# Attention of a fused two-layer mixer: the first query block in two visits of four heads per group, the second in four visits of two

## What is computed

```python
# 8 heads in 2 groups of 4, head width 64; one key and value head per group
q = rotary(zq) * Dh ** -0.5
p_c = masked_softmax(q @ k_c.T, mask_c) * mask_c          # 31 compressed keys
o_cmp = p_c @ v_c
# "selected" branch: 16 of 8 blocks, so all causal keys; "window" branch: window 512, so all causal keys
o_slc = softmax(q @ k_slc.T + causal) @ v_slc
o_win = softmax(q @ k_win.T + causal) @ v_win
g = sigmoid(zg)
o = g[..., 0:1] * o_cmp + g[..., 1:2] * o_slc + g[..., 2:3] * o_win
```

## Time and profile before

| | |
|---|---|
| median of three runs | 2074.64 us (2074.2 to 2075.43) |
| the profiled execution's own time | 2072.95 us |
| its span, first to last instruction | 2071.1 us |
| TensorE matmul busy | 2043.2 us, 99% of the span |
| VectorE busy | 1209.7 us, 58% |
| ScalarE busy | 685.6 us, 33% |
| GpSimd busy | 917.5 us, 44% |
| mean granted TensorE clock | 0.997 |

### The profile page before, as it was taken

One profiled execution on the slowest core, in us unless ns is written; L12 is line 12 of the kernel. 1 busy time (PEld: TensorE's weight loads), 2 busy tenths in 40 slices (PEclk: granted clock), 3 DMA queues, 4 the chain that ended last, 5 costly groups with the idle time before them and its releaser, 6 DMA issues.

```text
span 2071.1 us, 31913 instructions
## 1 busy us (share of the span) xinstructions
PE 2043.2 (99%) x9800; PEld 1637.2 (79%) x9800; DVE 1209.7 (58%) x1799; ACT 685.6 (33%) x1007; POOL 917.5 (44%) x672
## 2 busy tenths in 40 slices
PE   9999999999999999999999999999999999999997
PEld 7777677888888888888887777778888888888886
DVE  7766865422327888862267677572322378888522
ACT  4355533323232322222233554333323232222222
POOL 3422233444445555545544212335444455555552
PEclk9999999999999999999999999999999999999998
DMA  5311132222232223223233112322223223232233
GB/s 210 99 60 52 55 91 91 96 92 101 91 101 92 96 97 101 92 94 111 93 126 96 53 51 64 95 89 95 101 91 101 91 93 101 92 101 96 100 105 108
DMA packets 57432, 194.90 MB, mean 94 GB/s; under 512 B 7040, under 2 KB 7552, under 8 KB 57216
## 3 DMA queue, kind: packets, MB, share of 16 engines
q1 hardware_dynamic: 52576, 186.17, 26.8%
q10 hardware_dynamic: 4768, 7.61, 1.5%
HBM read 186.67 MB, written 2.10 MB: 91 GB/s over the span
## 4 chain that ended last, share of the span: by engine, by line
PE 93%; DVE 4%; issue 1%; ACT 1%; DMA 0%; ACTq 0%; SPq 0%; DVEq 0%
PE acc L1189 28%; PE acc L1191 28%; PE acc L1190 28%; PE o L1389 2%; PE s L1363 2%; PE t L1371 1%; PE o L1428 1%; PE s L1418 1%; PE t L1409 0%; DVE win_k L779 0%; DMA w_raw<-weights_dram 0%; PE s L1444 0%; PE s L1435 0%; DVE rstd L752 0%; DVE sc L721 0%
## 5 line engine op out<-in xcount | busy, mean ns | idle before, releaser
L434 POOL TENSOR_TENSOR w_lo<-w_raw,w_hi 128x512 fp32r<-128x512 f32 x668 | 917.3, 1394 | 1129.6 <-ACT w_hi L456 1114.0
L1189 PE MATMUL acc<-xg_hi,w_hi 128*128 128x512 f32 x1904 | 769.5, 404 | 6.5 <-DVE sc L721 3.6
L1191 PE MATMUL acc<-xg_hi,w_lo 128*128 128x512 f32 x1904 | 742.9, 390 | 0.0
L1190 PE MATMUL acc<-xg_lo,w_hi 128*128 128x512 f32 x1904 | 741.8, 390 | 0.0
L456 ACT ACTIVATE w_hi<-w_raw 128x1024 fp32r<-128x1024 f32 x336 | 355.1, 1057 | 777.5 <-PE acc L1191 740.3
L1189 PEld LDWEIGHTS acc<-xg_hi,w_hi 128*128 128x128 f32 x1904 | 357.4, 188 | 116.5 <-issue 33.4
L1190 PEld LDWEIGHTS acc<-xg_lo,w_hi 128*128 128x128 f32 x1904 | 357.8, 188 | 77.1 <-issue 6.7
L1191 PEld LDWEIGHTS acc<-xg_hi,w_lo 128*128 128x128 f32 x1904 | 357.3, 188 | 76.4
L1066 DVE TENSOR_TENSOR work<-acc,rstd 128x512 f32<-128x512 f32 x64 | 44.1, 690 | 256.1 <-PE acc L1191 256.1
L1189 PE MATMUL acc<-act_hi,w_hi 128*128 128x512 f32 x352 | 136.9, 389 | 0.0
L1190 PE MATMUL acc<-act_lo,w_hi 128*128 128x512 f32 x352 | 136.9, 389 | 0.0
(11 more groups left out here) (208 smaller groups left out, 2238.1 us busy)
## 6 DMA issues: line engine op xcount, KB each, us to landing
w_raw<-weights_dram SPq DMA_DIRECT2D x339, 512.0 KB, 3.3
x<-xT_dram SPq DMA_DIRECT2D x8, 256.0 KB, 5.9
rot<-rq ACTq DMA_DIRECT2D x16, 128.0 KB
rot<-rk ACTq DMA_DIRECT2D x16, 128.0 KB
dec<-decay_dram ACTq DMA_DIRECT2D x8, 256.0 KB, 3.3
out_dram<-x SPq DMA_DIRECT2D x8, 256.0 KB, 2.7
con<-consts_dram SPq DMA_DIRECT2D x1, 1406.0 KB, 10.5
w1k<-w_dram SPq DMA_DIRECT2D x2, 512.0 KB, 8.7
```

The costliest lines, as they stand in the source:

```text
L434: nc.gpsimd.tensor_tensor(w_lo[:, slot, part], w_raw[:, slot, part], w_hi[:, slot, part].bitcast(F32), ALU.subtract).then_inc(lo_ready, 1)
L1189: mm(tile, w_h, right_hi, start=first, stop=False)
L1190: mm(tile, w_h, right_lo, start=False, stop=False)
L1191: return mm(tile, w_l, right_hi, start=False, stop=last)
```

## The change

The pairs of one head give way to `VISITS`, each with a list of heads `js`. Block 0 has two visits of four heads per group, block 1 four visits of two, blocks 2 and 3 eight visits of one as before: 22 visits a layer, where there were 32. The steps of a visit are 4 slots apart in block 0, 3 in block 1, 2 in blocks 2 and 3. A group's heads lie side by side in one bank, so one `s` bank, one `t` bank and one copy to `pT` serve up to 512 columns. The count of products, transposes, exponentials and scalings stays, that of VectorE's copies and of its gate steps falls. `scores` on TensorE now waits for both banks before its first product. The last attention step moves from slot 73 to slot 62.

```diff
+VISITS = [(_qi, _br, tuple(range(_j, _j + _n))) for _qi, _n in ((0, 4), (1, 2), (2, 1), (3, 1))
+          for _j in range(0, 4, _n) for _br in range(2)]
+STEP = {0: 4, 1: 3, 2: 2, 3: 2}
...
-    if _n == 0:
-        _e += [("scores", 0), ("scores", 1)]
-    if _n % 2 and _n < UNITS:
-        _e.append(("scale", _n - 1))
-    if _n % 2 and 3 <= _n < UNITS + 2:
-        _e += [("turn", _n - 3), ("turn", _n - 2)]
-    if _n % 2 and _n >= 5:
-        _e.append(("values", _n - 5))
-    if _n % 2 and _n + 1 < UNITS:
-        _e += [("scores", _n + 1), ("scores", _n + 2)]
+STEP_SLOT = [4]
+for _qi, _, _ in VISITS:
+    STEP_SLOT.append(STEP_SLOT[-1] + STEP[_qi])
+STEP_SLOT += [STEP_SLOT[-1] + 2, STEP_SLOT[-1] + 4]
+for _i, _n in enumerate(STEP_SLOT):
+    if _i < len(VISITS) and (_i == 0 or VISITS[_i][0] != VISITS[_i - 1][0]):
+        _qi = VISITS[_i][0]
+        _at = _n + (0 if _qi else 1)
+        SIDE[_at].append(("cmp_scores", _qi))
+        SIDE[_at + 2].append(("cmp_scale", _qi))
+        SIDE[_at + 4].append(("cmp_turn", _qi))
+    if 1 <= _i <= len(VISITS):
+        SIDE[_n].append(("scale", _i - 1))
+    if 2 <= _i <= len(VISITS) + 1:
+        SIDE[_n].append(("turn", _i - 2))
+    if 3 <= _i:
+        SIDE[_n].append(("values", _i - 3))
+        if _i == len(STEP_SLOT) - 1 or VISITS[_i - 2][0] != VISITS[_i - 3][0]:
+            SIDE[_n].append(("attn_hi", VISITS[_i - 3][0]))
+            SIDE[_n + 2].append(("attn_lo", VISITS[_i - 3][0]))
+    if _i < len(VISITS):
+        SIDE[_n].append(("scores", _i))
...
-        def pr_of(u):
-            return (pr, pr_odd)[u // 2 % 2][:, u % 2, 0:(unit(u)[0] + 1) * P]
+        def pr_of(v, g):
+            return (pr, pr_odd)[v % 2][:, g, :]
...
-                                u = e[1]
-                                act.wait_ge(s_free, 1 + s_use(L, e) + 1)
-                                nc.scalar.activation(pr_of(u), pr_of(u), ACT.Exp, bias=nmax[:, u % 2:u % 2 + 1], scale=-1.0,
-                                                     accum_out=den[:, u % 4:u % 4 + 1]).then_inc(a_made, 1)
+                                qi, _, js = VISITS[e[1]]
+                                w = (qi + 1) * P
+                                for g in range(KV_GROUPS):
+                                    act.wait_ge(s_free, 1 + s_use(L, (*e, g)) + 1)
+                                    for i in range(len(js)):
+                                        part, c = pr_of(e[1], g)[:, i * w:(i + 1) * w], g * len(js) + i
+                                        ins = nc.scalar.activation(part, part, ACT.Exp, bias=nmax[:, c:c + 1], scale=-1.0,
+                                                                   accum_out=den[:, c:c + 1])
+                                    ins.then_inc(a_made, 1)
...
-                    u = e[1]
-                    w = (unit(u)[0] + 1) * P
-                    s_wait(e)
-                    alone(dve)
-                    s_end(ve.tensor_tensor_reduce(pr_of(u), s_of(e)[:, 0:w], C("causal", S)[:, S - w:S],
-                                                  -(DH ** -0.5), 3e38, ALU.add, ALU.min, nmax[:, u % 2:u % 2 + 1]), e)
+                    qi, _, js = VISITS[e[1]]
+                    w = (qi + 1) * P
+                    for g in range(KV_GROUPS):
+                        name = (*e, g)
+                        s_wait(name)
+                        alone(dve)
+                        for i in range(len(js)):
+                            c = g * len(js) + i
+                            ins = ve.tensor_tensor_reduce(pr_of(e[1], g)[:, i * w:(i + 1) * w], s_of(name)[:, i * w:(i + 1) * w],
+                                                          C("causal", S)[:, S - w:S], -(DH ** -0.5), 3e38, ALU.add, ALU.min, nmax[:, c:c + 1])
+                        s_end(ins, name)
 
                 def scale(e):
 
-                    u = e[1]
-                    qi, br, j = unit(u)
-                    sums, out_ = den[:, u % 4:u % 4 + 2], scl[:, u % 4:u % 4 + 2]
-                    dve.wait_ge(a_made, a_count(L, ("scores", u + 1)))
-                    then(ve.reciprocal(out_, sums))
-                    g2 = gates[:, qi, :].rearrange("p (g h b) -> p b h g", g=2, b=3)[:, 1 + br, j, :]
-                    v_end(ve.tensor_tensor(out_, out_, g2, ALU.mult), e)
+                    qi, br, js = VISITS[e[1]]
+                    n = KV_GROUPS * len(js)
+                    out_ = scl[e[1] % 2][:, 0:n]
+                    dve.wait_ge(a_made, a_count(L, ("scores", e[1], 1)))
+                    then(ve.reciprocal(out_, den[:, 0:n]))
+                    g2 = gates[:, qi, :].rearrange("p (g h b) -> p b g h", g=2, b=3)[:, 1 + br, :, js[0]:js[0] + len(js)]
+                    out3 = out_.rearrange("p (g h) -> p g h", g=2)
+                    v_end(ve.tensor_tensor(out3, out3, g2, ALU.mult), e)
 
                 def turn(e):
-                    u = e[1]
-                    w = (unit(u)[0] + 1) * P
-                    t_wait(e)
-                    if u >= 2:
-                        dve.wait_ge(pv_done, pv_count(L, ("values", u - 2)))
-                    t_end(ve.tensor_copy(pT[:, u % 2, 0:w], t_of(e)[:, 0:w]), e)
+                    qi, _, js = VISITS[e[1]]
+                    w = (qi + 1) * P * len(js)
+                    for g in range(KV_GROUPS):
+                        t_wait((*e, g))
+                        if e[1]:
+                            dve.wait_ge(pv_done, pv_count(L, ("values", e[1] - 1, g)))
+                        t_end(ve.tensor_copy(pT[:, g, 0:w], t_of((*e, g))[:, 0:w]), (*e, g))
...
-                    qi, br, h = unit(e[1])
+                    qi, br, js = VISITS[e[1]]
                     w = (qi + 1) * P
-                    r = slice(64 * (h // 4), 64 * (h // 4) + 64)
-                    b = s_begin(e)
+                    banks = [s_begin((*e, g)) for g in range(KV_GROUPS)]
                     last_wait()
-                    mm(b[:, 0:w], qT[r, h % 4, qi * P:(qi + 1) * P], kT[r, br, 0:w], start=True, stop=True).then_inc(s_done, 1)
+                    for i, j in enumerate(js):
+                        for g in range(KV_GROUPS):
+                            r = slice(64 * g, 64 * g + 64)
+                            ins = mm(banks[g][:, i * w:(i + 1) * w], qT[r, j, qi * P:(qi + 1) * P], kT[r, br, 0:w], start=True, stop=True)
+                            if j == js[-1]:
+                                ins.then_inc(s_done, 1)
...
+                    for g in range(KV_GROUPS):
+                        pe.wait_ge(a_made, a_count(L, ("scale", e[1], g)))
+                        b = t_begin((*e, g))
+                        last_wait()
+                        for k in range((qi + 1) * len(js)):
+                            ins = nc.tensor.transpose(b[:, k * P:(k + 1) * P], pr_of(e[1], g)[:, k * P:(k + 1) * P], ident)
+                        ins.then_inc(t_done, 1)
...
+                    for i, j in enumerate(js):
+                        products = [(v_nat[:, br, k, :], pT[:, :, i * w + k * P:i * w + (k + 1) * P]) for k in range(qi + 1)]
+                        if br == 1:
+                            products.append((vcz[:, j, :], cmp_pT[:, qi % 2, :, :]))
+                        for k, (v, p) in enumerate(products):
+                            for half in range(2):
+                                d = slice(DH * half, DH * half + DH)
+                                ins = mm(o_bank[qi % 2][d, j * P:(j + 1) * P], v[:, d], p[:, half, :],
+                                         start=(br == 0 and k == 0 and (len(js) == 1 or i == 0)), stop=(br == 1 and k == qi + 1),
+                                         skip_group_check=True)
+                                if j == js[-1] and k == len(products) - 1:
+                                    ins.then_inc(pv_done, 1)
```

More of the change, by code:

```diff
@@ L132 @@
             SIDE[4 * (_b + 2) + (1 if B_TILES[_b][0] == "rq" else 0) + _k].insert(0, ("rotate", B_TILES[_b], _k))
-for _qi in range(QT):
-    SIDE[UNIT_SLOT + 16 * _qi + 19].append(("attn_hi", _qi))
-    SIDE[UNIT_SLOT + 16 * _qi + 21].append(("attn_lo", _qi))
 SEQUENCE = [_e for _slot in SIDE for _e in _slot]
 S_USES = ["sumsq1", "hid_k", "hid_v", "kc", "vc", "kc_swap"]
-S_USES += [_e for _e in SEQUENCE if _e[0] in ("gate", "cmp_keys", "cmp_scores", "scores", "ret_scores", "ret_var", "pool")]
+S_USES += [_x for _e in SEQUENCE if _e[0] in ("gate", "cmp_keys", "cmp_scores", "scores", "ret_scores", "ret_var", "pool") for _x in ([(*_e, 0), (*_e, 1)] if _e[0] == "scores" else [_e])]
 S_USES += ["sumsq2"]
@@ L143 @@
 for _e in SEQUENCE:
-    if _e[0] in ("turn", "cmp_turn", "ret_turn"):
+    if _e[0] in ("cmp_turn", "ret_turn"):
         T_USES.append(_e)
+    if _e[0] == "turn":
+        T_USES += [(*_e, 0), (*_e, 1)]
 assert len(S_USES) % 2 == 0 and len(T_USES) % 2 == 0
@@ L151 @@
     for _e in _slot:
```

(23 more changed lines are left out.)

50 lines of the change are left out of this document (18 added, 32 removed).

## The result

The changed kernel takes 2078.32 us (median of 13 runs, 2075.05 to 2079.37), the kernel before, on the same chip, 2073.87 us (13 runs, 2072.24 to 2077.26). The ratio is 1.0021, with a 95% interval of 1.0014 to 1.0029. It is slower, by 4.4 us, where 8.6 us less were forecast. The profiled execution took 2078.32 us.

A forecast was written before the change was run, and what follows sets the result against it. TensorE bounds the kernel, its matmuls busy 2043.2 of 2071.1 us. Fewer visits -12.2, cleared stalls -7.6 and new waits +11.2 sum to -8.6, so 2074.64 becomes 2066.0 us; range 2059.5 to 2072.5.

The forecast's parts named there:

- The fixed price of a visit: Each attention visit costs TensorE 0.61 us whatever its width, for three changes of array division; twenty fewer visits give -12.2 us.
- rival C: Score products of merged visits don't chain: 4.2 us less saved, 2070.2 us; chance 0.13.
- the three added waits: New TensorE waits in slot 12, slot 28 and slot 44: 5.6 us a layer, +11.2 us, bounds +3.6 and +19.4.
- slot 44: TensorE waits for VectorE's copy of `cmp_pT` before the second group's transposes: 3.9 us, bounds 1.6 and 6.0.
- slot 28: As slot 44, with no convolution ahead: a TensorE wait of 0.5 us, bounds 0 and 1.5.
- slot 12: Score products wait for a bank, VectorE doing the first retention key's rotation before `cmp_scores`: 1.2 us, bounds 0.2 and 2.2.
- (2): Four old TensorE stalls for VectorE per layer, in slots 5, 9, 57 and 69, all cleared: 3.78 a layer, -7.6 us.
- slot 69: `ret_values` waits 1.22 us for the first product with `dec`; cleared, or up to 1.22 kept if means alone delay VectorE.
- slot 9: Old stall of 0.41 us where `cmp_turn` and `turn` stand together; cleared, since `cmp_turn` then stands alone.
- D: Rival: added stalls at their upper bounds, +19.4 us, giving 2074.2 us; chance 0.11.
- E: Rival: ScalarE's wide visits delay the weights' split, so TensorE's tiles start late: +20 us, 2086; chance 0.04.

## Why the prediction was wrong

**What held.** The fixed price of a visit, 0.61 us: two kernels in the old slots gave -11.1 and -5.5 us where twenty and twelve visits with their changed waits give -10.7 and -5.5, and by the length of stage B the price is 0.59 us in both. The Trainium skill, page "TensorEngine Tiling (Array Packing)", section "Key Properties", says that a change of tiling mode drains TensorE; that fewer changes with the same products save this much agrees with it. No run tells the changes of mode from anything else that a visit has once. Score products chain: 1.09 us for sixteen records where 1.06 was said and near 1.7 would have spoken for rival C. The sum of the three added waits was right: 11.2 us forecast, 10.8 measured (2.01, 0.19 and 3.20, and 1.98, 0.19 and 3.20), with slot 44 at 3.20 for 3.9, slot 28 at 0.19 for 0.5 and slot 12 at 2.0 for 1.2, near its upper bound. That the sum came out so near is luck: two terms were too high and one too low. Slot 12 was mis-sized because VectorE didn't begin the tile free: it read the sum of the tile before at 106.50 us, 2.0 us behind the new tile's first product, where the text had it done by 0.95, and after two rotation steps of quiet length it reached the compressed scores only at 108.63. In slot 44 the working was right as well: VectorE took 200.12 - 185.60 = 14.5 us from the compressed scores to the copy where near 15 was said, 1.50 of them in a wait for ScalarE's copy, said 1.4. In stage B of the changed kernel TensorE doesn't wait for `w_lo`, and for `acc` only at its start, as before.

**The step that failed: (2), slot 69, booked as cleared.** The sentence "in slots 63 to 69 no attention is left" was true and was read the wrong way round. The visits there were not only VectorE's load; for TensorE they were the cover under which VectorE made the means. The timeline of VectorE after the change, from the tile that holds the last average's input to the first head's product:

```profile
252.45 0.69 DVE L729 TENSOR_TENSOR sc<-acc,rstd 128x512 f32<-128x512 f32 x1
253.37 1.56 DVE L1042 TENSOR_TENSOR sc<-sc 128x511 f32<-128x511 f32 x1
254.97 1.14 DVE L1041 COPY sc<-sc 128x2 f32<-128x2 f32 x1
...
259.88 1.73 DVE L1048 SCALAR_TENSOR_TENSOR pool_early<-sc 128x512 f32<-128x512 f32 x1
261.73 0.69 DVE L729 TENSOR_TENSOR rq<-acc,rstd 128x512 f32<-128x512 f32 x1
262.64 0.69 DVE L964 TENSOR_TENSOR pr<-s,dec 128x512 f32<-128x512 f32 x1 [0.22 <-DVE rq L729]
```

VectorE is at work for 262.64 - 252.45 = 10.2 us without attention before it begins the head's first product. TensorE has only the stream and the head's first scores meanwhile and is ready for that head's product at 263.57 - 2.68 = 260.89 us. In the old slots TensorE had visits of block 3 beside the same steps, 5.93 - 2.72 = 3.21 us each. The wait grew from 1.22 to 2.68 us, above the bound of 1.22 that the text gave; with the blocks in their old slots it was 1.44, and with the average moved away 0.29. With slot 9, which kept 0.82 and 0.16 us, step (2) took away 7.6 - 5.4 - 1.0 = 1.2 us net and not 7.6.

**The term that was missing: the granted clock.** The sum priced a wait at its length. In stage B of before no wait is longer than 1.6 us and none has a fall behind it. One row of that trace could have warned, near the end of the span; the first line is from the timeline, the other two from the view by stretches:

```profile
2059.05 1.83 PE L1529 MATMUL s<-con,ssq 128*128 128x1 f32 x8 [2.41 <-DVE ssq L1088]
...
2056.00:2058.00 2.00, 0.65 (x3) 0.19 (x1) 0.69 (x1) 0.35 (x1) 0.00 (x0) 1.00 0.00 0
2058.00:2060.00 2.00, 0.95 (x5) 0.95 (x5) 1.56 (x3) 1.98 (x3) 0.00 (x0) 0.78 0.00 0
```

There the clock falls behind a wait of 2.41 us, and three added waits of up to 3.9 us were forecast. TensorE has little left to do at that place, so the row couldn't say what a fall costs in the stream. Four falls at 1.7 us are 6.8 us, and the term stood at nothing. The Trainium skill, page "TensorE: Matmul & The Clock Gate", section "HAM oscillation — how this bites in real kernels", says that waits between bursts of matmuls can put TensorE back to its lower clock each time; by that rule the clock had to be asked about as soon as a wait of 3.9 us was forecast, and the runs agree with it: all twelve waits of 3.64 us and more have a fall, and shorter ones have it too.

**The sum as it was.** -12.2 for the visits, -7.6 for the old stalls, +10.8 for slots 12, 28 and 44, +5.4 for slot 69, +1.0 for slot 9, +6.8 for the clock: +4.2 us, measured +4.4 by the medians and +4.7 by the length of stage B. Outside stage B, where no change to a tenth of a microsecond was said, the profiled span is 0.7 us longer: 1.1 more ahead of it, 0.5 less behind. The stretch ahead of it takes 77.0 to 78.7 us in the fourteen kernels, which are the same there. No rival had this: D put the added waits at their upper bounds but left slot 69 at nothing, and its 2074.2 was too low. E was not seen: in stage B TensorE doesn't wait for `w_lo`.

**Which is the cause of the loss.** The merging isn't it; alone it is worth 11 us. The moving forward of blocks 1 to 3 cost the rest, some 16 us (2078.32 against 2062.12, or 15.5 if each is held against its own kernel before), 14.4 of them in stage B: waits (17.2 - 9.9 = 7.3 us, small ones counted) and the clock (6.8). That is shown twice, by leaving the blocks where they were and by repairing the dense order. What stays open: why a wait of 2.0 us brings a fall in half of the cases and one of 3.2 in six of eight; and which place for the last average costs nothing. Both places tried brought waits of their own (3.69, or 1.2 and 0.5 us), as did the head's own move (3.67).

## What to carry to other kernels

A step that is taken out from between two engines takes its cover away with it: before a stall is booked as removed, ask what each engine still has to do there without the step, and for how long. Where two changes come together, here fewer visits and an earlier place for them, cost them apart; the first was worth 11 us and the second gave it all back. A wait of TensorE is priced at its length only while it is short: from 2 us on, put in the clock.

## What was unexpected of the hardware

In stage B TensorE's granted clock fell to 0.50 at 32 of 42 waits of 1.98 us and more, and at none of 36 waits of 1.1 to 1.8 us. In the changed kernel a fall costs 1.7 us, about as much as the shortest wait that brings one; but five of the 32 were twice as long, at waits of 3.2 us and more (in the run with the first head two slots later the stretches from 1310 to 1316 us are at 0.50 throughout). The falls differ from layer to layer with the same wait, and so a kernel with such waits should be timed more often: the times of one with four falls spread over 6.5 us, the longest at the lowest mean clock. Those of another with four spread over 1.7 us, so the number of falls in the profiled execution doesn't tell the spread.
